# Expert weights loaded by stage into a ring of four stages, in place of 19 single pieces

## The chip, the cores and the metric

The kernel runs on one core of one Trainium2 chip. The metric is the device time of one execution in microseconds (us), the median of several runs. In the profile PE is TensorE, PEld its weight loads, DVE is VectorE, ACT is ScalarE, POOL is GpSimd and SP is SyncE, whose queue issues most transfers. A "q" behind a name (SPq, PEq) is that engine's sequencer.

## The reference

One layer of a hybrid decoder on 256 new tokens and 8 single-token samples, 1024 channels, all in float32. A mixer (retention and an RWKV-7 recurrence, merged by gates) comes first; the change does not touch it. Behind it stands a mixture of experts, cut here to its core:

```python
# 4 groups of 8 experts, D_EXPERT = 256, TOP_K = 2
g_logit = xf @ router_group_w + router_group_b          # group: top 1
e_logit = xf @ router_expert_w + router_expert_b        # expert in the group: top 2
combine = ...                                           # (T, 32) weights, two of them not zero
h = silu(einsum('td,edf->tef', xf, expert_w_gate)) * einsum('td,edf->tef', xf, expert_w_up)
h = h * combine[..., None]
y = einsum('tef,efd->td', h, expert_w_down)
x = x + y;  out = rmsnorm(x, norm_final)
```

Each of the 32 experts has three matrices (gate and up 1024 x 256, down 256 x 1024) of 1 MB (1,048,576 bytes), 96 MB in all. Each is read once, as long as no expert has more than 32 tokens in a round.

## The kernel before, in words

The program has two phases. `mixer_phase` computes norm, mixer and residual; `moe_phase` (line 1374) is the one that changes. They share no buffer that matters here: the ring of the weights is allocated when the second phase begins.

The 32 experts are worked in eight quads of four (`QE = 4`, `NQ = 8`). A quad has three stages, gate, up and down, of four pieces each: 24 stages, 96 pieces. A piece is one matrix of one expert, 8 KB on each of 128 partitions.

**Loading.** SP issues everything from one queue. After five small transfers for the router it runs `load_round` (line 1450): pieces 0 to 95 in order, piece j into place `j % 19` of a ring of 19 places. Two conditions hold it back. The last two places hold, until the router's logits are computed, the transposed tokens `xnt` and the gain `gffn`, so that piece 17 waits for `logit_mm`. And from piece 19 on, piece j waits until TensorE has finished the stage that held the place before: `stage_done >= (j - 19) // 4 + 1`. Each place has a semaphore of its own (`piece_in0` to `piece_in18`).

**TensorE** (lines 1497 to 1615). It transposes the tokens, computes the logits (line 1517) and the positions of the tokens at their experts (lines 1527 to 1530), and then goes into the loop over the quads. For quad q it runs `gate_up` for gate and then for up (line 1567; 64 matmul records for each stage), the scatter of the quad before (line 1597), `weights_by_slot` (line 1550) and `gather` (line 1539) for the next quad, `turn_h` (line 1575), and `down` (line 1587). Ahead of the loop stand the gather and the slot weights of quad 0, behind it the scatter of quad 7. Each of the three weight stages begins with `landed` (line 1553), which waits for the semaphores of its four pieces, and ends by raising `stage_done`, which frees the stage's places for SP.

**The others.** VectorE routes (lines 1700 to 1755), builds the one-hot matrices, and adds what is scattered to x (line 1776). ScalarE and VectorE empty TensorE's banks. At the end `norm_final` is loaded into the place of piece 1 of the ring, and lines 1805 to 1811 scale the rows, which SP stores. The case of more than 32 tokens at an expert repeats the whole round; these inputs need one round.

Of the kernel before, what the change touches and what calls it, by code (L numbers as in the profile page):

```python
# [14 lines left out]
P = 128  # L15
# [17 lines left out]
QE = 4  # L33
# [131 lines left out]
def hybrid_moe_step(nc, a, o, k):  # L165

    w_in = a["w_in"][0].rearrange("(k p) c -> p k c", p=P)

    with ExitStack() as top:
        keep = {}  # L170

        def alloc(ctx, table, name, shape, dt=F32):
            table[name] = ctx.enter_context(nc.sbuf_tensor(name, shape, dt))
            return table[name]

        sem = Semaphores(nc)

        psum = [top.enter_context(nc.psum_tensor(f"bank{n}", [P, 512], F32)) for n in range(8)]
        cst = {}
        for n in ("ident", "tri", "ones", "slot"):  # L180
            alloc(top, cst, "c_" + n, list(k[n].shape))

        x = alloc(top, keep, "x", [P, 3, D])
        xn = alloc(top, keep, "xn", [P, 3, D])
        stat = alloc(top, keep, "xstat", [P, 3, 4])
        eps = alloc(top, keep, "eps", [P, 4])

        mixer_phase(nc, a, o, k, w_in, alloc, sem, psum, cst, keep)
        sem.next_phase()
        moe_phase(nc, a, o, k, alloc, sem, psum, cst, keep)  # L190
        sem.next_phase()
# [1182 lines left out]
def moe_phase(nc, a, o, k, alloc, sem, psum, cst, keep):  # L1374
# [5 lines left out]
    with ExitStack() as ctx:  # L1380
        sb = {}

        def buf(name, shape, dt=F32):
            return alloc(ctx, sb, name, shape, dt)
# [2 lines left out]
        x, xn, stat, eps = keep["x"], keep["xn"], keep["xstat"], keep["eps"]  # L1387

        PIECE = KT * DE
        RING = 19  # L1390
        STAGES = 3 * NQ
        PIECES = QE * STAGES
        ring = buf("ring", [P, RING * PIECE])
        FIRST_LATE = RING - 2
        late = ring[:, FIRST_LATE * PIECE:]
        xnt = late[:, 0:KT * T].rearrange("p (k t) -> p k t", k=KT)
        gffn = late[:, KT * T:KT * T + D]

        assert all(j % RING != 1 for j in range(PIECES - 3 * QE, PIECES))
        gfin, junk_end = ring[:, PIECE:PIECE + D], ring[:, PIECE + D:PIECE + 2 * D]  # L1400

        ysb = buf("ysb", [P, D])
# [38 lines left out]
        def place(j):  # L1441
            return ring[:, (j % RING) * PIECE:(j % RING + 1) * PIECE]

        def loads_before(j):

            return j // RING + 1, -(-(PIECES - j % RING) // RING)

        with nc.Block() as block:

            def load_round(sp, rnd):  # L1450
                first = isinstance(rnd, int)
                if not first:
                    sp.wait_ge(sem("stage_done"), rnd * STAGES)
                for j in range(PIECES):
                    q, m, i = j // (3 * QE), j // QE % 3, j % QE
                    if first and j == FIRST_LATE:
                        sp.wait_ge(sem("logit_mm"), 1)
                    if j >= RING:
                        sp.wait_ge(sem("stage_done"), rnd * STAGES + ((j - RING) // QE + 1))
                    src = a[("expert_w_gate", "expert_w_up", "expert_w_down")[m]][0, q * QE + i]  # L1460
                    sp.dma_start(place(j).rearrange("p (k f) -> p k f", f=src.shape[-1]),
                                 src.rearrange("(p k) f -> p k f", p=P)).then_inc(sem(f"piece_in{j % RING}"), 16)

            @block.sync
            def _(sp):
                sp.dma_start(gffn[0:B, :], a["norm_ffn"].partition_broadcast(B)).then_inc(sem("gffn_in"), 16)
                sp.dma_start(rw[:, :, 0:NG], a["router_group_w"][0].rearrange("(p k) c -> p k c", p=P)).then_inc(sem("rw_in"), 16)
                sp.dma_start(rw[:, :, NG:NG + NE], a["router_expert_w"][0].rearrange("(p k) c -> p k c", p=P)).then_inc(sem("rw_in"), 16)
                sp.dma_start(rb[:, 0:NG], a["router_group_b"].partition_broadcast(P)).then_inc(sem("rw_in"), 16)
                sp.dma_start(rb[:, NG:NG + NE], a["router_expert_b"].partition_broadcast(P)).then_inc(sem("rw_in"), 16)  # L1470
                load_round(sp, 0)
                sp.wait_ge(sem("rounds_ready"), 1)
                n_rounds = sp.value_load(rounds_i[0:1, 0:1], min_val=1, max_val=MAX_ROUNDS)
                with sp.If(n_rounds > 1):
                    with sp.Fori(1, n_rounds) as rnd:
                        load_round(sp, rnd)
                sp.wait_ge(sem("last_quad"), n_rounds)
                sp.dma_start(gfin, a["norm_final"].rearrange("(o d) -> o d", o=1).partition_broadcast(P)).then_inc(sem("gfin_in"), 16)
                for tt in range(TT):
                    sp.wait_ge(sem("y_final"), tt + 1)  # L1480
                    sp.dma_start(o["y_p"][0].rearrange("(t p) d -> p t d", p=P)[:, tt, :], xn[:, tt, :]).then_inc(sem("y_sent"), 16)
                sp.wait_ge(sem("y_final"), 3)
                sp.dma_start(o["y_s"].rearrange("b t d -> (b t) d"), xn[0:B, 2, :]).then_inc(sem("y_sent"), 16)
                sp.wait_ge(sem("y_sent"), 48)
# [12 lines left out]
            def _(pe):  # L1497
# [26 lines left out]
                for tt in range(3):  # L1524
                    m = SIZE[tt]
# [25 lines left out]
                    last.then_inc(sem("swt_mm"), 1)  # L1551

                def landed(rnd, stage):
                    for i in range(QE):
                        nth, a_round = loads_before(stage * QE + i)
                        pe.wait_ge(sem(f"piece_in{(stage * QE + i) % RING}"), rnd * (16 * a_round) + 16 * nth)

                def gate_up(rnd, n, q, m):
                    stage = 3 * q + m
                    if m == 0:  # L1560
                        pe.wait_ge(sem("xg_copy"), 2 * n + (2 + AHEAD["xg_copy"]))
                        pe.wait_ge(sem("sw_copy"), n + 1)
                        pe.wait_ge(sem("hx_done"), n + AHEAD["hx_done"])
                    landed(rnd, stage)
                    for kk in range(KT):
                        for i in range(QE):
                            last = mm((GB, UB)[m][quad(i), 0:DE], xg[q % 2][:, kk, quad(i)], place(stage * QE + i)[:, kk * DE:(kk + 1) * DE],  # L1567
                                      start=(kk == 0), stop=(kk == KT - 1))
                    last.then_inc(sem("stage_done"), 1)
# [8 lines left out]
                def down(rnd, n, q):  # L1578
                    stage = 3 * q + 2
                    pe.wait_ge(sem("hT_copy"), n + (1 + AHEAD["hT_copy"]))  # L1580
                    pe.wait_ge(sem("y_copy"), 2 * n + AHEAD["y_copy"])
                    landed(rnd, stage)
                    for hf in range(2):
                        for f in range(DE // P):
                            for i in range(QE):
                                at = f * D + hf * 512
                                last = mm(YB[hf][quad(i), :], hT[:, f, quad(i)], place(stage * QE + i)[:, at:at + 512],  # L1587
                                          start=(f == 0), stop=(f == DE // P - 1))
                        last.then_inc(sem("stage_done" if hf else "y_half"), 1)
# [253 lines left out]
```

## Time and profile before

| | |
|---|---|
| time, 3 runs | median 947.8 us (947.59 to 948.4) |
| the profiled execution: time / span | 949.6 us / 947.9 us |
| mean granted TensorE clock | 0.934 of full speed |
| busy: PE / PEld | 840.9 us (89%) / 604.8 us (64%) |
| busy: DVE / ACT / POOL | 432.1 us (46%) / 219.6 us (23%) / 70.6 us (7%) |
| HBM read / written | 158.68 MB / 8.43 MB |

The span runs from the first to the last instruction of the profiled execution; its whole time is 1.7 us longer. A busy share is an average over phases with different limits. The mixer takes the span up to about 675 us; the MoE phase takes the rest, and in it 96 pieces of 1024 KB are loaded. A slice of the page is 947.9 / 40 = 23.7 us.

### The profile page before, as it was taken

To read this page: it belongs to the slowest core of one execution; us is meant where nothing else is said; L and a number is where in the kernel's file an instruction comes from. 1 tells how busy PE (TensorE), PEld (TensorE's weight loads), DVE (VectorE), ACT (ScalarE), POOL (GpSimd) and SP (SyncE) were. 2 spreads that over 40 slices of the span, in tenths; PEclk is the share of its full clock that TensorE was granted. 3 is DMA by queue.
4 is the path that set the end of the run, shared out by engine and by line. 5 is a ranking of instruction groups with operands and counts; after the bars stand their busy time and mean duration, and the time that the engine had idled before them with its cause. 6 is when DMAs were issued, how large, how long until landed. Compare 5 with 4: busy or idle time off the path is not lost. (4 is left out here: it accounts for less than half of the span.)

```text
span 947.9 us, 14552 instructions
## 1 busy us (share of the span) xinstructions
PE 840.9 (89%) x5559; PEld 604.8 (64%) x5559; DVE 432.1 (46%) x960; ACT 219.6 (23%) x445; POOL 70.6 (7%) x69
## 2 busy tenths in 40 slices
PE   3599999999999999999999997974669999999985
PEld 2367787787787787877976876631356564555441
DVE  3133564555555556547546546886230212322314
ACT  3121422423414404405314322101100000000002
POOL 0000000000000000000000003990000000000000
PEclk9889999999999999999999998995756999999998
DMA  9934323324224223224124223012399999999992
GB/s 275 233 88 115 111 68 93 89 66 123 71 75 115 66 66 115 66 66 137 44 68 136 76 80 131 1 68 93 102 421 400 419 418 419 418 419 418 418 407 77
DMA packets 108512, 167.61 MB, mean 177 GB/s; under 512 B 7505, under 2 KB 91691, under 8 KB 95804
## 3 DMA queue, kind: packets, MB, share of 16 engines
q1 hardware_dynamic: 104780, 158.96, 47.4%
q0 software_dynamic: 1664, 4.98, 1.4%
q10 hardware_dynamic: 2032, 3.18, 1.2%
q8 instruction: 24, 0.39, 0.2%
q14 instruction: 12, 0.10, 0.0%
HBM read 158.68 MB, written 8.43 MB: 176 GB/s over the span
## 5 line engine op out<-in xcount | busy, mean ns | idle before, releaser
L274 PE MATMUL bank<-room,wall 128*128 128x264 f32 (+1 forms) x1152 | 291.7, 400 | 26.2 <-ACT thw L792 14.1
L274 PEld LDWEIGHTS bank<-room,wall 128*128 128x128 f32 x1152 | 214.9, 194 | 74.0 <-issue 19.1
L1539 PE MATMUL bank<-G,xn 128*128 128x128 f32 (+1 forms) x384 | 74.6, 328 | 3.0 <-DVE G L1760 3.0
L1539 PEld LDWEIGHTS bank<-G,xn 128*128 128x128 f32 (+1 forms) x384 | 56.9, 204 | 19.3 <-issue 6.5
L1567 PE MATMUL bank<-ring,xg 128*32 128x256 f32 x1024 | 61.1, 399 | 4.3 <-DMA ring<-in_expert_w_up_dram 3.4
L1567 PEld LDWEIGHTS bank<-ring,xg 128*32 128x32 f32 x1024 | 36.2, 115 | 30.5 <-issue 13.0
L274 PE MATMUL bank<-wall,merged 128*128 128x512 f32 (+1 forms) x96 | 45.2, 619 | 2.7 <-DVE merged L1312 2.5
L1597 PE MATMUL bank<-ysb,SW 128*128 128x512 f32 (+1 forms) x96 | 45.6, 610 | 1.0 <-DVE ysb L1799 1.0
L1587 PE MATMUL bank<-ring,hT 128*32 128x512 f32 x256 | 35.8, 710 | 4.9 <-ACT hT L1655 4.9
L1776 DVE TENSOR_TENSOR x<-x,bank 128x512 f32<-128x512 f32 (+1 forms) x48 | 32.8, 684 | 14.7 <-PE bank L1597 14.7
L1769 DVE COPY xg<-bank 128x512 f32<-128x512 f32 x8 | 5.5, 691 | 71.8 <-PE bank L1539 71.8
L1110 POOL DMA_DIRECT2D out_rwkv_p_dram<-zout x8 | 4.9, 617 | 411.9 <-ACT zout L835 411.2
L274 PE MATMUL bank<-xn,a 128*128 128x128 f32 (+1 forms) x192 | 32.6, 313 | 0.0
L274 PEld LDWEIGHTS bank<-wall,merged 128*128 128x128 f32 (+1 forms) x96 | 14.6, 159 | 27.0 <-issue 23.2
L1597 PEld LDWEIGHTS bank<-ysb,SW 128*128 128x128 f32 (+1 forms) x96 | 11.8, 155 | 31.2 <-DVE x L1776 22.6
L274 PEld LDWEIGHTS bank<-xn,a 128*128 128x128 f32 x192 | 28.7, 194 | 2.9 <-issue 0.5
L1021 DVE TENSOR_SCALAR zst<-bank,epc 128x64 f32<-128x64 f32 x32 | 9.0, 281 | 43.8 <-PE bank L274 43.8
L1587 PEld LDWEIGHTS bank<-ring,hT 128*32 128x32 f32 x256 | 9.3, 126 | 25.7 <-issue 22.1
L767 ACT ACTIVATE mshift<-bank,pt 128x272 f32<-128x272 f32 x24 | 11.7, 489 | 52.1 <-PE bank L274 52.1
L1640 ACT COPY xg<-bank 128x512 f32<-128x512 f32 x8 | 4.7, 585 | 78.3 <-PE bank L1539 78.3
L274 PE MATMUL bank<-x 128*128 128x128 f32 x128 | 17.4, 294 | 4.1 <-DVE x L923 4.1
L1799 DVE COPY ysb<-bank 128x512 f32<-128x512 f32 x8 | 5.5, 692 | 33.4 <-PE bank L1587 33.4
(364 smaller groups left out, 1311.8 us busy)
## 6 DMA issues: line engine op xcount, KB each, us to landing
wall<-in_w_in_dram SPq DMA_DIRECT2D x72, 512.0 KB, 3.9
ring<-in_expert_w_gate_dram SPq DMA_DIRECT2D x32, 1024.0 KB, 26.5
ring<-in_expert_w_up_dram SPq DMA_DIRECT2D x32, 1024.0 KB, 19.7
ring<-in_expert_w_down_dram SPq DMA_DIRECT2D x32, 1024.0 KB, 26.1
room<-in_state_ret_dram SPq DMA_DIRECT2D x8, 512.0 KB, 4.8
out_ret_s_dram<-room POOLq DMA_DIRECT2D x8, 512.0 KB, 3.4
wall<-in_w_out_dram SPq DMA_DIRECT2D x8, 512.0 KB, 3.5
room<-in_state_rwkv_dram SPq DMA_DIRECT2D x1, 2048.0 KB, 8.5
```

The costliest lines, as they stand in the source:

```text
L274: return nc.tensor.matmul(out, lhsT, rhs, start=start, stop=stop, skip_group_check=loose)
L767: A.activation(mshift[m][:, 1:TX + 1], pj[use % 2][:, 0:TX], ACT.Copy, scale=pt[:, PX["mu_" + nm]:PX["mu_" + nm] + 1]).then_inc(sem(f"mu_{ ...
L1021: V.tensor_scalar(zst[c][:], M[4 + par_][:, t * P + HD:(t + 1) * P], epc[:, c:c + 1], None, mult).then_inc(sem(f"state{c}"), 1)
L1110: eng.dma_start(o["rwkv_p"][0, 0].rearrange("h v k -> v h k")[:, bass.ds(n * 2 - 2, 2), :], zout[:]).then_inc(sem("zout_sent"), 16)
L1539: last = mm(XG[kk // 4][:, (kk % 4) * P:(kk % 4 + 1) * P], xn[rows(tt), tt, kk * P:(kk + 1) * P], G[q % 2][rows(tt), tt].rearrange("p e s ...
L1567: last = mm((GB, UB)[m][quad(i), 0:DE], xg[q % 2][:, kk, quad(i)], place(stage * QE + i)[:, kk * DE:(kk + 1) * DE], start=(kk == 0), stop= ...
L1587: last = mm(YB[hf][quad(i), :], hT[:, f, quad(i)], place(stage * QE + i)[:, at:at + 512], start=(f == 0), stop=(f == DE // P - 1))
L1597: mm(SB[hf][rows(tt), :], SW[q % 2][:, cols(tt)], ysb[:, hf * 512:(hf + 1) * 512], start=True, stop=True).then_inc(sem("scat_mm"), 1)
L1640: A.copy(xg[q % 2][:, 0:4, :], XG[0][:].rearrange("p (k s) -> p k s", k=4)).then_inc(sem("xg_copy"), 1)
L1769: V.tensor_copy(xg[q % 2][:, 4:8, :], XG[1][:].rearrange("p (k s) -> p k s", k=4)).then_inc(sem("xg_copy"), 1)
L1776: V.tensor_tensor(x[rows(tt), tt, hc], x[rows(tt), tt, hc], SB[hf][rows(tt), :], add).then_inc(sem("scat_add"), 1)
L1799: V.tensor_copy(ysb[:, 512:1024], YB[1][:, :]).then_inc(sem("y_copy"), 1)
```

## The change

The ring becomes one of four stages (16 places, 16 x 8 KB on each partition instead of 19 x 8 KB). One transfer loads the four matrices of a stage, 4 MB, with one semaphore for each of the four slots. The slot of stage s is `s % 4`; stage s waits, from stage 4 on, for `stage_done >= s - 3`. The late room (`xnt`, `gffn`) moves into slot 3, whose first load, that of stage 3, waits for `logit_mm`. TensorE's `landed` waits for one semaphore instead of four. The arithmetic, its order, and the places of the pieces within a stage stay as they are.

```diff
         PIECE = KT * DE
-        RING = 19
+        RING = 4 * QE
         STAGES = 3 * NQ
...
-        FIRST_LATE = RING - 2
+        FIRST_LATE = RING - QE
         late = ring[:, FIRST_LATE * PIECE:]
...
+        STAGE_SLOTS = RING // QE
...
-        def loads_before(j):
-
-            return j // RING + 1, -(-(PIECES - j % RING) // RING)
-
...
-                for j in range(PIECES):
-                    q, m, i = j // (3 * QE), j // QE % 3, j % QE
-                    if first and j == FIRST_LATE:
+                for stage in range(STAGES):
+                    q, m = stage // 3, stage % 3
+                    slot_ = stage % STAGE_SLOTS
+                    if first and stage * QE == FIRST_LATE:
                         sp.wait_ge(sem("logit_mm"), 1)
-                    if j >= RING:
-                        sp.wait_ge(sem("stage_done"), rnd * STAGES + ((j - RING) // QE + 1))
-                    src = a[("expert_w_gate", "expert_w_up", "expert_w_down")[m]][0, q * QE + i]
-                    sp.dma_start(place(j).rearrange("p (k f) -> p k f", f=src.shape[-1]),
-                                 src.rearrange("(p k) f -> p k f", p=P)).then_inc(sem(f"piece_in{j % RING}"), 16)
+                    if stage >= STAGE_SLOTS:
+                        sp.wait_ge(sem("stage_done"), rnd * STAGES + (stage - STAGE_SLOTS + 1))
+                    src = a[("expert_w_gate", "expert_w_up", "expert_w_down")[m]][0, q * QE:(q + 1) * QE]
+                    room = ring[:, slot_ * QE * PIECE:(slot_ + 1) * QE * PIECE]
+                    sp.dma_start(room.rearrange("p (e k f) -> p e k f", e=QE, f=src.shape[-1]),
+                                 src.rearrange("e (p k) f -> p e k f", p=P)).then_inc(sem(f"stage_in{slot_}"), 16)
...
                 def landed(rnd, stage):
-                    for i in range(QE):
-                        nth, a_round = loads_before(stage * QE + i)
-                        pe.wait_ge(sem(f"piece_in{(stage * QE + i) % RING}"), rnd * (16 * a_round) + 16 * nth)
+                    nth, a_round = stage // STAGE_SLOTS + 1, STAGES // STAGE_SLOTS
+                    pe.wait_ge(sem(f"stage_in{stage % STAGE_SLOTS}"), rnd * (16 * a_round) + 16 * nth)
```

## Rows read from the trace of the kernel before

**Rows 1.** The page's 40 slices: busy tenths, granted clock, DMA share, GB/s.

```profile
PE   3599999999999999999999997974669999999985
PEclk9889999999999999999999998995756999999998
DMA  9934323324224223224124223012399999999992
GB/s 275 233 88 115 111 68 93 89 66 123 71 75 115 66 66 115 66 66 137 44 68 136 76 80 131 1 68 93 102 421 400 419 418 419 418 419 418 418 407 77
```

**Rows 2.** The chain that ended last, from 880 us: start, us, what.

```profile
889.99 26.43 DMA ring<-in_expert_w_up_dram
916.41 0.14 issue
916.55 4.93 PE bank L1567 x64
...
928.16 3.68 PE bank L1587 x32
```

**Rows 3.** The timeline of TensorE: start, us, operation, records, idle before and its releaser.

```profile
722.13 10.00 PE L1567 MATMUL bank<-ring,xg 128*32 128x256 f32 x128 [0.89 <-issue]
...
745.53 7.09 PE L1567 MATMUL bank<-ring,xg 128*32 128x256 f32 x128
...
827.54 7.09 PE L1567 MATMUL bank<-ring,xg 128*32 128x256 f32 x128
...
909.50 3.64 PE L1567 MATMUL bank<-ring,xg 128*32 128x256 f32 x64
916.55 4.93 PE L1567 MATMUL bank<-ring,xg 128*32 128x256 f32 x64 [3.41 <-DMA ring<-in_expert_w_up_dram]
```

**Rows 4.** Windows of the MoE phase: busy by engine, granted clock, DMA share, GB/s.

```profile
682.00:684.00 2.00, 0.00 (x0) 0.00 (x0) 0.00 (x0) 0.00 (x0) 0.00 (x0) 0.50 0.86 357
684.00:720.00 36.00, 27.31 (x122) 23.13 (x122) 9.39 (x57) 0.42 (x2) 0.00 (x0) 0.50 1.01 421
720.00:728.00 8.00, 7.11 (x61) 3.72 (x64) 0.69 (x1) 0.96 (x2) 0.00 (x0) 0.50 1.01 418
728.00:732.00 4.00, 4.00 (x76) 2.27 (x68) 0.42 (x1) 0.38 (x1) 0.00 (x0) 1.00 0.84 303
732.00:922.00 190.00, 182.28 (x1569) 98.42 (x1566) 46.75 (x77) 15.60 (x35) 0.00 (x0) 0.96 1.01 419
922.00:926.00 4.00, 4.00 (x10) 1.02 (x8) 2.72 (x4) 0.00 (x0) 0.00 (x0) 1.00 0.50 209
...
926.00:926.50 0.50, 0.50 (x2) 0.11 (x2) 0.23 (x2) 0.00 (x0) 0.00 (x0) 1.00 0.00 0
```

**Rows 5.** SP's timeline, the issues of expert weights around the first release.

```profile
678.54 2.35 SPq L1461 DMA_DIRECT2D ring<-in_expert_w_gate_dram  x4
...
699.86 29.20 SPq L1461 DMA_DIRECT2D ring<-in_expert_w_up_dram  x4
729.11 3.41 SPq L1461 DMA_DIRECT2D ring<-in_expert_w_down_dram  x4
```

**Rows 6.** Line 1461 in 700 to 734: issue ns min/median/max, first and last start.

```profile
L1461 SPq DMA_DIRECT2D ring<-in_expert_w_up_dram x4: 328/2142/3499, 699.9 to 728.7; - x4
```

**Rows 7.** The timeline of VectorE where the logits are done.

```profile
693.83 0.39 DVE L1702 TENSOR_TENSOR lg<-bank,rb 128x36 f32<-128x36 f32 x3 [1.22 <-PE bank L1517]
```

**Rows 8.** Line 1556, the waits of `landed` in TensorE's sequencer: ns min/median/max.

```profile
L1556 PEldq EVENT_SEMAPHORE  x56: 51/51/51, 722.0 to 926.4; - x56
```

**Rows 9.** Transfers by size: KB each, us to landing; then line 1461 alone.

```profile
wall<-in_w_out_dram SPq DMA_DIRECT2D x8, 512.0 KB, 3.5
room<-in_state_rwkv_dram SPq DMA_DIRECT2D x1, 2048.0 KB, 8.5
...
DMA to landing us min/median/max: 5.5/24.6/28.8
```

## The prediction, made before the kernel was run

> **What bounds the kernel now.** I read the page's 40 slices first [rows 1]. Up to slice 27 the DMA engines are two to four tenths busy; from slice 28 (the MoE phase) they stand at 9 and move 418 to 421 GB/s until slice 37, with TensorE at 9 as well. Two resources are full at once, so the second view has to say which one ends last: the chain, read from its end [rows 2]. It passes through TensorE work and then through one transfer, the up weights of the last quad (a quad is a group of four experts), issued at 889.99 and landed 26.43 us later at 916.41. Up to there TensorE had been busy: in the timeline of TensorE [rows 3] the gate stage of the last quad ends at 909.50 + 3.64 = 913.14, then comes the idle of 3.41 us with the landing as its releaser. In no other quad does a landing show as releaser. So the stream of expert weights sets the end, but TensorE is only 3.41 us ahead of it; and what follows the landing (the up matmuls, scatter, down, scatter, norm, 947.9 - 916.4 = 31.5 us) hangs on it in full.
>
> Third, the stream itself, in windows [rows 4]: 357 GB/s in 682 to 684, 421 up to 720, 418 up to 728, 303 in 728 to 732, 419 up to 922, then the engines run out one after another, and at 926 nothing is left. One piece is 1024 KB = 1.049 MB, 2.50 us at 419. The one gap, at 728 to 732, costs 4 x (419 - 303) / 419 = 1.1 us. Its cause is in SP's own timeline [rows 5]: the issue of four up pieces begun at 699.86 lasts to 729.06; with the shortest issue of 0.328 us its last one starts at 728.7 [rows 6]. That is piece 19, the first that must wait for a released place. The release is the first gate stage, which TensorE begins at 722.13 [rows 3], since it first has to route and gather, and does at half clock.
>
> So 19 places are just about as much as the stream fills before TensorE lets go of the first place.
>
> **The change part by part.**
>
> *Depth, 19 pieces to 16.* Pieces 0 to 15 can be loaded ahead of the first release; pieces 16 to 18, which now go out before it, wait for it. Moved by 720: 2 x 357 + 36 x 421 GB/s = 15.87 MB [rows 4]. Sixteen pieces are 16.78 MB, so the new stream runs dry at 720 + 0.91/0.418 = 722.2. Nineteen are 19.92 MB, by the same count 729.7, and with the gap of 1.1 us the old stream goes on as from 730.8. The release comes at the same time in both kernels, since nothing ahead of it depends on the loads (stage 0 landed long before 722). The new one therefore idles 730.8 - 722.2 = 8.6 us instead of 1.1: **+7.5 us**, which is three pieces of 2.50 us. Nothing gives them back: total bytes are the same and the old stream has no other gap. The cover that hid them, a prefetch of 19 against a first release at 728.7, is exactly what goes.
>
> *Later stages.* Does the four-slot ring stall again? Stage s may load when stage s - 4 is done. Loads restart at 730.8 and a stage takes 10.0 us. Stage 5 needs the first up stage, done at 732.1, while stage 4 streams to 740.8: in time. Stage 6 needs the first down stage, done at 745.7, while stage 5 streams to 750.9: 5.1 us early, the tightest case, against about 2 us from an issue to packets (728.7 to 730.8). From there TensorE gains on the stream: from the gate stage of quad 1 (745.53) to that of quad 7 (909.50) it takes 27.3 us a quad, against 30.0 for twelve pieces [rows 3]. So no second stall, 0 us. If that cover were gone (over 5 us from issue to packets) each quad would lose the excess.
>
> *TensorE between.* Restarted at 730.8, the up weights of quad 1 land at 740.8 and those of each quad after it 30.0 us later: of quad 4 at 830.9 or a little after, for the slowest engine. TensorE asks for them at 827.54 + 3.5 = 831.0: from quad 4 or 5 on it waits in every quad, some 2 us, and about 4 in the last. These waits lie beside the stream and move nothing, as the releases stay ahead. They may halve the granted clock for a stretch: behind the 3.41 us idle the up stage took 4.93 us against 3.64 for the gate stage before it [rows 3]. In before that is paid once on the path, after the last landing, and I expect the same again, 0 us; both ends: -1.3 (full clock) and +1.3 (one more such stretch).
>
> *The first loads.* The last slot now holds what the router needs, so twelve pieces instead of seventeen go out before the logits are done. They end by 693.83 [rows 7]; twelve pieces, 12.6 MB, last to about 684 + 11.9/0.421 = 712.2. The condition has 18 us to spare: 0 us. The four SP issues per stage shrink to one; SP is ahead of the queue and not on the path.
>
> *Four waits to one in TensorE's queue.* A wait instruction is 51 ns [rows 8], 72 are gone. Once the stream bounds, they are hidden by it. Ahead of the first gate stage three go, at most 0.15 us earlier release: **-0.15 us**. Should TensorE bound instead, all 72 are 3.7 us.
>
> *A 4 MB transfer in place of four.* The trace has no transfer of 4 MB. Nearest by size [rows 9]: 512 KB land in 3.5 us, of which 1.25 are data at 419; 2048 KB in 8.5, data 5.0. The part that is not data grows from 2.2 to 3.5 us; a ring piece at its shortest, 5.5, gives 3.0. Carried on in a line from 512 KB over 2048 KB, 4096 KB have 5.2, that is 2.2 us over a single piece; the other end is 0, if that growth is only the engines' unequal ends, which the old stream already shows (922 to 926). It is paid once at the restart and at the last landing, not per stage, since stages queue behind each other. I take **+0.3 us**, near the lower end, because four pieces issued together already land only with the slowest engine. The rate itself: 419 stays; 421, as up to 720, would give -1.0 us.
>
> The down weights of the last quad drain by 926.0 and are wanted at 928.16 [rows 2, 4]; both shift together, so they stay 2 us early.
>
> Sum: 7.5 - 0.15 + 0.3 = +7.65 us. Span 947.9 to 955.6. The profiled execution took 949.6 (1.7 outside the span), so 957.2; the median of the runs shown, 947.8, is 1.8 lower, so **955.4 us** (+0.8%).
>
> **Rivals.**
>
> *The stream gets faster with large transfers and the kernel ends earlier.* Place: the 80 pieces after 730.8, 200 us at 419. To make up 7.65 us the rate must be 3.9% higher, 436 GB/s; at 440 it would be 190.6 us and the median 945.8. The floor is TensorE's chain: without its wait (3.41), the slow stretch (1.3) and the 3.7 us of waits 947.8 - 8.4 = 939.4. For it speaks only that fewer transfers mean fewer ends; against it, that pieces are queued 24.6 us deep (median to landing [rows 9]), that no row of any length has more than 421, and that the DMA share reads 1.01. Chance 0.06; landing within 0.2% of before, by a rate of 432 to 440, 0.03. The Trainium skill ("DMA: Bandwidth & Descriptors", section "Bandwidth") says to batch DMAs to 1 MiB or more and gives 78% of peak at 1 MB, 97% at 16 MB; by it the stream would speed up and this rival would win down to its floor. The trace disagrees: 1 MB pieces, back to back, run at 419.
>
> *The stream gets slower.* A stage transfer goes partition by partition through four experts, so neighbouring stretches of the source lie 1 MB apart instead of 8 KB. Each per cent of rate costs 2.0 us on the 200 us; at 5% less the time is 965.9, at half the rate it is 1155. No transfer of the trace has such a pattern; against a loss speaks that each stretch stays 8 KB long. Chance 0.07. [...]
>
> *The ring stalls again* (issue to packets over 5 us, or slots released late): up to 2 us in each of the first quads, 958 to 963. Against it the 5.1 us of margin. Chance 0.07.
>
> *The forecast* has 0.77. Its own range: low with full clock behind the last landing (-1.3) and 421 GB/s (-1.0), 953.0; high with +1.9 more for the large transfer and one more slow stretch (+1.3), 958.6. The range given, 952.7 to 959.5, takes in part of the second stall. Two tenths of a per cent, 1.9 us, is about what a measurement of this kernel can tell from no change: faster 0.06, same 0.03, slower 0.91.
>
> **What the new profile would show.** A gap in the DMA slices at about 722 to 731 of 8 to 9 us and none later; 419 GB/s around it; the first gate stage still at 722; landings named as releaser of the up stages from quad 4 on, about 2 us each and 4 in the last; the last up landing at about 924; the span from there 31.5 us. Wrong if the gap is there but the rate after it differs by over 1%, if TensorE waits at gate or down stages, or if the first release moves.

## The result, and the profile after

The changed kernel takes 951.5 us (median of 6, 949.5 to 954.5) against 947.7 us of the kernel before beside it: ratio 1.0049, 95% interval 1.0025 to 1.0072. Measured once more (e10) it is 1.0047 (1.0024 to 1.0070). So it is slower, by about 4.5 us or 0.5%. The forecast was slower by 7.65 us, 955.4; the measured 951.5 lies below its range (952.7 to 959.5), and 7.65 is just outside both intervals (2.3 to 6.8 us).

The page of the profile after, its 40 slices; to be read beside [rows 1]:

```profile
span 947.8 us, 14424 instructions
PE   3599999999999999999999997975669999899895
PEclk9899999999999999999999998996657999989999
DMA  9934324224224224124224233022497999999992
GB/s 268 239 99 125 89 67 125 71 74 115 66 66 120 61 66 137 44 68 136 66 68 135 66 83 116 1 69 92 164 422 299 418 421 420 419 419 420 418 419 97
```

One slice inside the stream is new: 299 GB/s after 422. The windows show it as a gap at the place that was forecast (answers to [rows 4]; same columns):

```profile
682.00:684.00 2.00, 2.00 (x11) 2.00 (x11) 0.00 (x0) 0.00 (x0) 0.00 (x0) 0.50 0.99 414
...
716.00:720.00 4.00, 3.31 (x25) 1.78 (x29) 0.69 (x1) 0.96 (x2) 0.00 (x0) 0.50 0.59 244
720.00:724.00 4.00, 4.00 (x68) 2.15 (x64) 0.02 (x1) 0.38 (x1) 0.00 (x0) 0.82 0.00 0
724.00:728.00 4.00, 4.00 (x64) 2.26 (x53) 0.82 (x2) 0.38 (x1) 0.00 (x0) 1.00 0.83 303
...
736.00:920.00 184.00, 170.13 (x1484) 87.88 (x1487) 45.79 (x75) 15.08 (x34) 0.00 (x0) 0.96 1.01 419
...
922.00:926.00 4.00, 4.00 (x10) 1.11 (x9) 2.69 (x5) 0.00 (x0) 0.00 (x0) 1.00 0.81 338
```

Against 419 GB/s these windows lack 1.7, 4.0 and 1.1 us: the stream stands still for 6.8 us, where the forecast has 8 to 9 (8.6 in its sum).

The span of this execution, 947.8 us, is that of the one before, 947.9. That is no contradiction: it is the fastest of its six, and its MoE phase began earlier. SP's first issue of the phase (the gain, line 1466) stands at 675.64 in the profile before and here, first row of this excerpt of SP's timeline (start, us, what), at 672.38. The second row is the first reuse of a place, so the first release:

```profile
672.38 0.30 SPq L1466 DMA_DIRECT2D ring<-in_norm_ffn_dram  x1
...
723.48 0.37 SPq L1461 DMA_DIRECT2D ring<-in_expert_w_up_dram  x1
```

The mixer ahead of it is the same code, yet its time differed by up to 5.6 us over the profiles of this study (phase start at 670.0 to 675.6; only e11, e12, e17 and e18 change anything in it, six small loads). All times from here on are therefore counted **from that first issue of the phase**. So counted, the MoE phase took 272.3 us before and 275.4 after: +3.2 us in this pair (differences are taken before rounding, here and below).

The chain and TensorE's timeline at the end (answers to [rows 2, 3]):

```profile
884.71 33.39 DMA ring<-in_expert_w_up_dram
918.11 0.04 issue
918.15 3.66 PE bank L1566 x64
...
928.42 3.69 PE bank L1586 x32
```

```profile
826.94 5.35 PE L1566 MATMUL bank<-ring,xg 128*32 128x256 f32 x64 [3.57 <-DMA ring<-in_expert_w_up_dram]
...
858.32 3.66 PE L1566 MATMUL bank<-ring,xg 128*32 128x256 f32 x64 [1.77 <-DMA ring<-in_expert_w_up_dram]
...
918.15 3.66 PE L1566 MATMUL bank<-ring,xg 128*32 128x256 f32 x64 [0.18 <-DMA ring<-in_expert_w_up_dram]
```

The last up landing is still what the end hangs on. It comes at 918.11 - 672.38 = 245.7 us instead of 916.41 - 675.64 = 240.8: +5.0 us, where +7.65 was forecast. Landings are the releaser of up stages from quad 3 on, 0.2 to 3.6 us. Behind some of them the up stage takes 5.35 us, behind others 3.66. Behind the last one it was 3.66 here and 4.93 before, and that chance gives back 1.3 us in this pair. The stages behind it took 0.5 us less, so that of the +5.0 at the landing +3.2 are left at the end. The forecast had such waits from quad 4 on, some 2 us each and about 4 in the last, which was 0.18.

### The profile page after: what moved, and what is told of

Its sections match the earlier page's. It is cut to its first block and busy times, and to the rows that moved or that the text cites. A ratio compares the mean times of both kernels' runs of the same rounds, so it can differ in the third digit from the quotient of the medians.

```text
span 947.8 us, 14424 instructions
## 1 busy us (share of the span) xinstructions
PE 836.0 (88%) x5559; PEld 599.4 (63%) x5559; DVE 431.4 (46%) x960; ACT 219.5 (23%) x445; POOL 70.7 (7%) x69
## 5 line engine op out<-in xcount | busy, mean ns | idle before, releaser
L274 PE MATMUL bank<-room,wall 128*128 128x264 f32 (+1 forms) x1152 | 288.4, 396 | 26.2 <-ACT thw L792 14.0
L274 PEld LDWEIGHTS bank<-room,wall 128*128 128x128 f32 x1152 | 212.7, 192 | 72.9 <-issue 19.1
L1566 PEld LDWEIGHTS bank<-ring,xg 128*32 128x32 f32 x1024 | 34.3, 116 | 40.5 <-DMA ring<-in_expert_w_up_dram 12.4
L1586 PE MATMUL bank<-ring,hT 128*32 128x512 f32 x256 | 32.4, 650 | 4.4 <-ACT hT L1654 4.4
L903 DVE RECIPROCAL yrs<-yrs 128x264 f32<-128x264 f32 x8 | 14.4, 1803 | 13.6 <-ACT yrs L778 13.6
```

The costliest lines, as they stand in the source:

```text
L274: return nc.tensor.matmul(out, lhsT, rhs, start=start, stop=stop, skip_group_check=loose)
L903: V.reciprocal(ors[:], ors[:]).then_inc(sem("o_inv"), 1)
```

## The experiments

Eighteen runs, each timed in five rounds beside the kernel before; a ratio is to that kernel, with its 95% interval. What the profiles show of them, from the first issue of the phase, in us ("release": issue into the first reused place; "landing": of the last up stage):

| kernel | places, transfer | ratio (interval) | router loads landed | release | landing |
|---|---|---|---|---|---|
| before / e9 again | 19, 1 MB | 1 / 0.9992 (0.9970, 1.0014) | 8.7 / 8.6 | 53.1 / 52.9 | 240.8 / 240.9 |
| changed / e10 again | 16, 4 MB | 1.0049 / 1.0047 | 8.2 / 6.2 | 51.1 / 49.3 | 245.7 / 243.9 |
| e1 | 16, 1 MB | 1.0068 (1.0041, 1.0095) | 8.2 | 52.6 | 247.4 |
| e2 | 18, 2 MB | 1.0008 (0.9988, 1.0028) | 8.4 | 52.9 | 243.1 |
| e3 / e4 late start | 19 / 16 | 1.0028 (1.0008, 1.0047) / 1.0061 (1.0038, 1.0084) | 6.9 / 6.1 | 50.4 / 49.8 | 241.6 / 244.4 |
| e5 / e6 less gather | 19 / 16 | 0.9995 (0.9981, 1.0010) / 1.0067 (1.0048, 1.0087) | 6.9 / 8.4 | 50.2 / 52.5 | 239.5 / 247.2 |
| e7 / e8 busy while routing | 19 / 16 | 1.0001 (0.9982, 1.0020) / 1.0022 (1.0002, 1.0043) | 9.6 / 7.1 | 53.1 / 49.9 | 242.1 / 244.5 |
| e11 / e12 early router loads | 19 / 16 | 0.9917 (0.9899, 0.9936) / 0.9972 (0.9953, 0.9991) | before the phase | 47.0 / 47.2 | 231.5 / 238.4 |
| e13 / e14 busy before the gather | 19 / 16 | 1.0000 (0.9975, 1.0025) / 1.0004 (0.9981, 1.0027) | 8.4 / 5.9 | 47.4 / 44.0 | 240.5 / 240.0 |
| e15 / e16 ring moved | 19 / 16 | 0.9946 (0.9925, 0.9967) / 1.0013 (0.9989, 1.0037) | 8.4 / 6.4 | 51.5 / 49.9 | 237.0 / 241.3 |
| e17 / e18 e11 + e13 | 19 / 16 | 0.9904 (0.9884, 0.9924) / 0.9902 (0.9888, 0.9916) | before the phase | 39.8 / 39.6 | 231.3 / no wait |

In each pair the kernel with 16 places loads 4 MB at a time. In the rows read for "release" of the 1 MB kernels, the last of four merged issues is taken, as in [rows 5, 6]. Each line rests on one profiled execution, the ratio on five to twelve.

**e1, depth alone.**

```diff
-        RING = 19
+        RING = 16
-        FIRST_LATE = RING - 2
+        FIRST_LATE = RING - QE
```

> The kernel before with one edit: a ring of 16 single pieces (and the late room in its last four places). Transfers stay 1 MB. Theory D (depth: the stream stands still from the 16th piece to the first release): slower than before by as much as the changed kernel, +3.8 us, with a gap of 7 to 9 us in the DMA. Rival G (the size of the transfers costs at restart and landing, depth is hidden): within 1 us of before. Rival O (large transfers gain something, depth costs the full 7.5 us): +6 to +7.5 us.

Measured: 952.9 us, +6.4 us (3.9 to 9.0). The gap is there with 1 MB transfers:

```profile
718.00:720.00 2.00, 1.77 (x7) 0.96 (x5) 0.69 (x1) 0.70 (x2) 0.00 (x0) 0.50 0.97 401
720.00:728.00 8.00, 7.33 (x84) 4.08 (x88) 0.23 (x1) 0.64 (x2) 0.00 (x0) 0.59 0.10 40
728.00:730.00 2.00, 2.00 (x44) 1.24 (x39) 0.19 (x1) 0.00 (x0) 0.00 (x0) 1.00 0.82 229
```

So depth, not grouping, makes the change slow. The forecast's size fits this kernel: its release is at 52.6, near that of before, its stream stands still for 8.2 us by these windows (forecast 8.6), and its landing is +6.6 us.

**e2, transfers of two experts, 18 places.**

```diff
-        RING = 19
+        RING = 18
...
+                    sp.dma_start(room.rearrange("p (e k f) -> p e k f", e=2, f=src.shape[-1]),
...
```

> Transfers of 2 MB (two experts) in nine slots, 18 places, norm_final into place 7. D: one place less than before is at most one piece time, +2.5 us, less what the earlier release gives back: 0 to +2 us. G: about half of what grouping by four costs, +2 us or more, with little gap in the DMA. O: 0 us or faster than before.

+0.8 us (-1.1 to +2.7), landing +2.3. The time alone does not exclude the 2 us of G. The stream does: from 726 to 731 us it moved 143 GB/s in the mean, which is 3.3 us of standstill against 1.1 before. That is one place, and G expected little gap.

**e3, e4, a later start of the stream.** In both kernels:

```diff
+                sp.wait_ge(sem("rw_in"), 64)
                 load_round(sp, 0)
```

> The kernel before, but SP waits for the four router loads to land before the first piece of weights goes out, some 5.5 us later. D: with 19 places there is no idle time in the stream to absorb it, so +4 to +5.5 us. If the stream's start does not matter (TensorE bounds): 0 us.

> The changed kernel with the same late start of the stream. D: the stream only fills the ring later, which was idle 7 us before the first release anyway: same as the changed kernel, +3.8 us against before, and the gap shrinks to some 2 us. If the late start costs in itself as in the other kernel: +8 to +9 us against before.

e3: +2.7 us, less than the 4 to 5.5 expected, though its stream starts 4.1 us later (6.95 against 2.90) and has no gap at all. Two things gave some back, and neither was in the expectation: with no weights beside them the router loads land 1.7 us earlier, and the gap of [rows 4] is gone. e4: +5.8 us, within the noise of the changed kernel's 4.5, for a start 3.2 us later: the idle ring takes it up, and the standstill shrinks to 3.8 us (some 2 were expected). Both agree with D in kind; the size of e3 is below what D gave.

**e5, e6, less work for TensorE** (the gather of quads 1 to 7 leaves out the eight sample tokens).

```diff
-                        for tt in range(3):
+                        for tt in range(2 if q else 3):
...
```

> The kernel before, with the gather of quads 1 to 7 left without its third part (the 8 sample tokens), which takes a third of its matmuls, some 2.8 us a quad, from TensorE. Theory M (the end of the kernel before is the later of two nearly equal chains, TensorE's and the stream's, so that in many executions TensorE sets it and a later stream costs only the excess): faster than before by 1 to 3 us, with a wait for the last up weights well above 3.4 us. Rival (the stream alone sets the end of the kernel before): no change within 0.5 us.

> The changed kernel with the same part of the gather left out. M: here TensorE waits in every quad already, so less work for it changes little (0 to -1 us against the changed kernel), and the distance to the light form of the kernel before is the whole 7 us of the stall. Rival (the small loss comes from the earlier first release or from the large transfers): the distance between the two light kernels stays at 4 to 5 us.

Theory M finds no support: e5 is not measurably faster (-0.5 us, -1.8 to +0.9, which still reaches into M's 1 to 3 us). Its profile speaks against M too: TensorE waits 6.32 us for the last up weights instead of 3.41, and they land at 239.5, hardly earlier. So it is the stream that sets the end. The distance between the two, 0.72% or 6.8 us, is larger than that of the full kernels, though within its noise; in e6's profile the release is as late as in before (52.5) and the landing at 247.2. This pair suggested where to look: not at TensorE's work, but at the release.

**e7, e8, TensorE busy while it waits during routing** (19 matmuls in three groups).

```diff
+                busy(8)
                 pe.wait_ge(sem("rw_in"), 64)
...
+                busy(7)
                 pe.wait_ge(sem("mask_ready"), 1)
...
+                busy(4)
```

> The kernel before, with 19 extra matmuls that only keep TensorE busy while it waits during routing (8 for the router's loads, 7 for the mask, 4 for the one-hot matrix). If the granted clock is full in the first gather and gate stage, the first release comes some 10 us earlier. D: the gap in the stream (1 to 2 us) goes, TensorE is 10 us more ahead of the stream: 1 to 3 us faster than before. If the clock stays at half: 0 to +1 us.

> The changed kernel with the same 19 matmuls. D: with a release 10 us earlier the ring of 16 does not run dry either (or by 1 us at most): the changed kernel gains 5 to 8 us and ends within 1 us of the warm form of the kernel before. G (large transfers cost something in themselves): it stays 2 us or more behind it. If the clock stays at half: the distance between the two stays at 4 to 7 us.

Missed its aim: the first gather took 15.05 us in both, as before, with the clock still at half. The distance is 2.0 us, less than the 4 to 7 that were expected for this case. In the profiles the release of e8 comes 3.2 us earlier than that of e7 (49.9, 53.1). By itself this is inconclusive.

**e9, e10, both kernels again, unchanged.**

> The kernel before, unchanged, as one of the kernels compared: its ratio to itself should be 1.000 within its interval, and its profile is a second look at the time of the first release, counted from the start of the MoE phase (53.1 us in the first profile). If that time varies by a us or more from execution to execution (theory V: the prediction was sized on an execution with a late release, and a ring of 19 has a stall only when the release is late), it should differ here.

> The changed kernel, unchanged, once more beside the others. D with V: +5 to +6.5 us against before, as the three other kernels with 16 places (+6.4, +5.8, +6.3 us); if the first measurement (+4.6) is its true distance because large transfers gain something: +3 to +4.5 us.

In all these profiles a release is read from one execution. The kernel before repeats its release (52.9). The changed one does not: 49.3 now, 51.1 first, and its landing follows (243.9, 245.7). Where the difference begins is in the chain, in the last of the router's loads (start, us; the rows of before, changed, and e10 in this order):

```profile
678.07 6.25 DMA rb<-in_router_expert_b_dram
```

```profile
674.82 5.72 DMA rb<-in_router_expert_b_dram
```

```profile
676.24 3.78 DMA rb<-in_router_expert_b_dram
```

From this landing to the gate stage little varies (37.8 us before, 36.6 in e10, whose logits took 6.07 us against 7.04). Of the twelve profiles with this order of loads and nothing added before the logits, three of five with 4 MB transfers have the router loads in before 7 us (e10, e14, e16) and one of seven with 1 or 2 MB transfers (e5). That points to large transfers letting the small ones ahead of them through sooner; with so few profiles it is not shown.

**e11, e12, router loads at the end of the mixer.** One of the four loads, at its new and its old place:

```diff
+            sp.dma_start(rw[:, :, 0:NG], a["router_group_w"][0].rearrange("(p k) c -> p k c", p=P)).then_inc(sem("router_in"), 16)
...
-                sp.dma_start(rw[:, :, 0:NG], a["router_group_w"][0].rearrange("(p k) c -> p k c", p=P)).then_inc(sem("rw_in"), 16)
```

> The kernel before, with the router's weights and biases loaded at the end of the mixer phase instead of ahead of the ring in SP's queue (two constant matrices move to ScalarE's queue in the MoE phase to make room). The stream starts 2.6 us earlier and without small transfers ahead of it, and the logits start some 5 us earlier. D: the stream of 19 places runs through without a stall, its last up landing comes 3 to 5 us earlier, and the kernel is 3 to 4 us faster than before, if TensorE follows; if TensorE's chain takes over: 2 to 3 us.

> The changed kernel with the same early router loads. D: the ring runs dry 3 to 4 us earlier, the release comes 5 us earlier, so the gap shrinks by 1 to 2 us and the last landing comes 5 us earlier: 4 to 5 us faster than the changed kernel, that is +0 to +2 us against before; the distance to the early form of before stays at 4 to 5.5 us, since the depth is the same.

Both gain more than expected: 939.2 us (-7.9) and 943.9 (-2.7 against before). The distance, 0.55% or 5.2 us, is as expected. The landing of e11 comes 9.3 us earlier, where the earlier start explains at most 5: the stream itself was faster. More than the loads changed in these two kernels: two constant matrices moved to ScalarE's queue, and the ring came to another address (e15).

**e13, e14, 13 matmuls ahead of the loop.** Meant to hold the release back:

```diff
+                for _ in range(13):
+                    mm(psum[7][:, 0:P], ident[:], ident[:], start=True, stop=True)
                 loop(pe, one_round)
```

> The kernel before with 13 extra matmuls of 128 columns ahead of the loop over the quads, which hold the first gather and with it the first release back by some 5 us. Theory V (release time): the ring of 19 now runs dry in every execution, for some 6 us: +4 to +5 us against before. If the release does not matter with 19 places: 0 us.

> The changed kernel with the same 13 matmuls. V: the ring of 16 runs dry for some 13 us, and the distance to the held form of before is the full price of three pieces, 7 to 7.5 us, so +11 to +12.5 us against before. If large transfers give something back: the distance stays at 4 to 6 us.

The opposite happened, in both. TensorE had no break ahead of the gather, and the granted clock went from half to full (in e14 between 698 and 702, in e13 at the gather's start). Windows of e14, then its timeline (each of the 13 matmuls has two records):

```profile
695.00:698.00 3.00, 3.00 (x16) 2.69 (x14) 1.03 (x8) 0.00 (x0) 0.00 (x0) 0.50 1.00 418
698.00:702.00 4.00, 4.00 (x24) 4.00 (x23) 2.20 (x5) 0.00 (x0) 0.00 (x0) 0.59 1.02 422
702.00:710.00 8.00, 8.00 (x49) 6.19 (x48) 0.00 (x0) 0.00 (x0) 0.00 (x0) 1.00 1.01 419
...
717.00:720.00 3.00, 3.00 (x64) 1.64 (x56) 0.42 (x1) 0.38 (x1) 0.00 (x0) 1.00 0.89 306
```

```profile
696.83 5.29 PE L1615 MATMUL bank<-c_ident 128*128 128x128 f32 x26
701.96 8.41 PE L1539 MATMUL bank<-G,xn 128*128 128x128 f32 x48
```

The gather takes 8.4 us (e13: 8.5) instead of 15.05 and the release comes at 44.0 (e13: 47.4), about when 16 places are full. The ring of 16 hardly runs dry (306 GB/s over 3 us, and 383 over the next 4, are what is left of the gap, 1.2 us), and **the two kernels are equal** within their intervals of a quarter of a per cent: 1.0000 and 1.0004, landings 240.5 and 240.0. Take the late release away, and no loss is left that can be measured. The kernel before gains nothing, since its ring bridges the wait either way. Two reservations: in the profiles the release of e14 is 3.4 us earlier than that of e13, and with e13's the ring of 16 would still have lost some 1.5 us (47.4 + 194.6 = 242.0; for the 194.6 see the next section); and a release held back on purpose, the experiment that was planned, was not run.

**e15, e16, the ring's address.** By the kernel's allocations, not by a trace, the ring begins at byte 43232 of each partition, 224 above a multiple of 256. In e11 and e12 the router's tiles ahead of it had moved it by 1312 bytes, to a multiple of 256. Now an unused tile of 32 bytes moves it, and all buffers behind it, to 43264, a multiple of 256 too:

```diff
+        buf("pad", [P, 8])
         ring = buf("ring", [P, RING * PIECE])
```

> The kernel before with an unused tile of 32 bytes per partition ahead of the ring. The ring then begins at a multiple of 256 bytes instead of at a multiple of 32 that is none of 64. Theory A (the rate of the stream hangs on the alignment of its destination): 426 to 427 GB/s, the last up landing 3.5 us earlier, 2 to 4 us faster than before. Rival (the rate came from something else in the early kernels, such as the small transfers that are gone): 419 GB/s and no change.

> The changed kernel with the same tile ahead of the ring. A: 427 GB/s, 3 to 4 us faster than the changed kernel, +0.5 to +1.5 us against before. Rival: 419 GB/s and +4.5 us.

Theory A holds: 940.5 us (-5.1, -7.1 to -3.1) and -3.3 us against the changed kernel. The same window of before, of e15 and of e11:

```profile
740.00:900.00 160.00, 156.22 (x1329) 82.27 (x1329) 44.10 (x72) 13.37 (x30) 0.00 (x0) 0.96 1.01 419
```

```profile
740.00:900.00 160.00, 151.85 (x1306) 83.37 (x1302) 42.38 (x69) 12.79 (x29) 0.00 (x0) 0.99 1.01 426
```

```profile
740.00:900.00 160.00, 154.34 (x1338) 83.98 (x1330) 43.09 (x70) 13.38 (x30) 0.00 (x0) 0.99 1.01 426
```

**e17, e18, early router loads and the 13 matmuls.** Diffs as in e11 and e13.

> The kernel before with the early router loads of e11 and the 13 matmuls of e13 ahead of the loop. The stream of e11 had no gap already and set the end, so an earlier release gives at most what TensorE's slow stretches still cost: 0 to -1.5 us against e11 (939.2 us), that is 7.5 to 9.5 us faster than before.

> The changed kernel with both. If the release is what closed the distance: the gap of 5 to 6 us of e12 shrinks to under 2 us, the last up landing comes within 1 us of that of e17, and the two kernels end within 1.5 us of each other, both some 8 us faster than before. If the closing in e13 and e14 had another cause: it stays 4 to 5 us behind e17.

937.5 and 936.4 us, against 946.0 of the kernel before beside them: 0.9904 and 0.9902. Here the two releases are alike, 39.8 and 39.6. In e18, the changed kernel, the gap is gone, and TensorE runs through the gate and up stages of the last quad without a wait. These are the best two kernels, 9.1 and 9.3 us faster than before, and between them 19 single pieces or four stages makes no difference that can be measured. This is the clean pair for the claim of e13 and e14.

## Why the prediction was wrong

**What bounds the kernel: right.** The stream sets the end before and after; e5 supports it, since less work for TensorE brings nothing that can be measured. The page was read loosely, without effect on the sum: its first two slices have a DMA share of 9 as well, and inside the stream one slice has 400 GB/s, which is the gap.

**Depth, 19 to 16: right in kind, and its price at an equal release right in size.** From the release to the last landing there are 73 pieces before and 76 after: 240.8 - 53.1 = 187.7 and 245.7 - 51.1 = 194.6 us. The second number returns in e10, e1, e4, e6 and e8 (194.6 to 194.8), the first in e9 (188.0), the other execution in which the ring of 19 ran dry. The difference, 7.0 us, stands where the forecast has 7.5.

**"The release comes at the same time in both kernels, since nothing ahead of it depends on the loads": this step failed.** In the profiled pair it came 2.0 us earlier in the changed kernel (51.1 against 53.1), and in e10 3.8 us. The forecast had named this itself as a sign of being wrong ("if the first release moves"). The standstill of the stream shows it once more: 8.6 forecast, less 2.0, is 6.6, and 6.8 were measured. The sum of the pair, from the phase's start: 7.0 for three pieces, -2.0 for the release, landing +5.0. I split the 2.0: router loads landed 0.5 earlier, the gap before the gate stage is 0.89 - 0.69 = 0.2 shorter (forecast: 0.15, for three waits; the row of the changed kernel stands below), and in the rest, 1.3, the clock rose to full earlier within the first gate stage (the gate and up stages together took 8.71 us against 10.00 in [rows 3]).

```profile
718.15 8.71 PE L1566 MATMUL bank<-ring,xg 128*32 128x256 f32 x128 [0.69 <-issue]
```

The step had two faults. Its reason is wrong: the router's loads are in flight until 684.3, while the first pieces are issued from 678.5 on [rows 5], and without weights beside them they land at 6.9 and 6.1 (e3, e4), against 8.4 to 8.7 in four of the five other profiles with 19 places in which they lie ahead of the ring and nothing is added before them. And it took one execution's release for the release. Ten profiles have the original order of loads and no matmuls added ahead of the gather (before, changed, e1, e2, e5, e6, e9, e10, e15, e16): in them the release lies between 49.3 and 53.1, and the one I took is the latest. A ring of 19 cannot gain from an early release beyond its gap of 1.1 us, and one of 16 gains from it until its own gap is closed: e13 and e14, e17 and e18 are the extreme cases, with equal times. A price read off one execution with a late release was therefore the upper end, not the middle. Two profiles of each kernel put the last landing 4.0 us later in the changed one (245.7 and 243.9 against 240.8 and 240.9), near the 4.5 us of the times.

How much of the mean difference is the loads and how much the clock stays open: e1, with 1 MB transfers and the same depth, is at +6.4 us against 4.5 for the changed kernel, but the intervals overlap (3.9 to 9.0; 2.3 to 6.8). Nor is it shown that the mean release of the changed kernel is earlier than that of the kernel before; there are two profiles of each.

**Later stages: right.** No second gap in any profile with 16 places. **TensorE between: right in kind,** with waits from quad 3 on, one quad earlier than forecast, but of 0.2 to 3.6 us, not of 2 each and 4 in the last. Its two ends were needed, and the upper one was a little short: the up stage behind the last landing took 3.66, 3.66 and 6.5 us (changed, e16, e10), against 4.93 before. **First loads, waits: right.** Stage 3 was issued at 690.04, long before the stream needed it.

**A 4 MB transfer in place of four: 0.3 us was charged, and none is seen.** From release to landing e1 takes 194.8 us with 1 MB and the changed kernel 194.6 with 4 MB. (The low end of the range, 955.4 - 1.3 - 1.0, is 953.1, not 953.0.) The rival of a slower stream (experts 1 MB apart in the source) did not occur, 419 GB/s in both. Nor did that of a faster one. The Trainium skill ("DMA: Bandwidth & Descriptors", section "Bandwidth") wants transfers of 1 MiB or more and shows 16 MB ones at a higher rate than 1 MB ones; here that makes no difference: pieces of either size, queued one behind another, keep the DMA share at 1.01.

## What to carry to other kernels

A prefetch ring in front of a saturated stream is worth what it bridges once, here at least: the time from its being full to the first release. So before changing its depth, work out that one time in several executions, not in one, and price the change at the spread; and look first at the release itself, which here was cheaper to move (13 otherwise useless matmuls, four small loads issued earlier) than three places of memory are worth. Once the release comes early enough, as in e17 and e18, 16 places and large transfers do as well as 19 and small ones.

## What the runs showed of the hardware that was not expected

**The address of the destination set the rate of the stream.** With the ring at 224 bytes past a multiple of 256 it was 418 or 419 GB/s from 740 to 900 us (420 in e6); at a multiple of 256, 426 or 427 (e11, e12, e15 to e18), 1.8% more, worth 3.2 us from release to landing (e16: 241.3 - 49.9 = 191.4 instead of 194.6) and, with what else varied, 5.1 us in e15. An unused tile of 32 bytes does it. The Trainium skill ("DMA: Bandwidth & Descriptors", section "How a descriptor splits into AXI transactions") says that a descriptor which does not start at a multiple of 256 bytes has its first transaction start at the boundary below, and that the unused bytes still cost beats. For 8 KB that begin 224 bytes above a boundary an estimate by that rule is 263 beats in place of 256, 2.7%. The page says this of the bytes read, and here it is the destination that moved; the runs agree in direction and have 1.8%. That the same rule is the cause is not shown, nor whether a multiple of 64 or 128 would do as well.

**The clock in the first gather could be bought.** It was at half, 1.2 GHz (gather 15.05 us), in every kernel in which TensorE paused ahead of it, for 3.0 us or, in e7 and e8, for 1.0, and at full, 2.4 GHz (8.4 to 8.5 us), in the four kernels in which TensorE was busy from the position matmuls through (e13, e14, e17, e18). Once at half it stayed there long: in the kernel before TensorE works through 15.05 us of gather, and the granted clock is 0.50 until 728 [rows 4].

**The granted clock behind a wait for a landing is not the same each time:** behind waits of 0.2 to 1.8 us the up stage took 3.66 us, behind waits of about 3.0 and 3.6 us it took 3.66 in some cases (e12, e3) and 5.35 in others (e11, e2). Executions of one kernel differ by up to 9 us (the kernel before: 941.5 to 950.7 in 28 runs), twice the effect that was to be explained. How much of that is the clock, the release or the length of the mixer is not shown.
